# Embedding stages that multiply the unnormalized input, the next stage's sums of squares taken inside them, two normalizations in a row joined, and rotary angles computed behind the scaling

## The reference

```python
for i in range(DEPTH):                                   # 2 layers
    ...                                                  # layer 0: pooling; layer 1: attention (nsa)
    x = x + conv_ffn(rmsnorm(x, norm_ffn[i]), ...)
    gate = jax.nn.sigmoid(rmsnorm(x, norm_ple[i]) @ ple_gate[i])     # 1024 x 1024
    x = x + gate * (p[i] @ ple_proj[i])                  # p[i]: 256 tokens x 256, ple_proj: 256 x 1024
return rmsnorm(x, norm_final)

def rmsnorm(x, g):
    xf = x.astype(jnp.float32)
    y = xf * lax.rsqrt(jnp.mean(xf * xf, axis=-1, keepdims=True) + EPS) * g.astype(jnp.float32)
    return y.astype(x.dtype)
```

## Time and profile before

| | us |
|---|---|
| median of three runs | 2557.86 (2557.30 to 2558.94) |
| the profiled execution, its time | 2558.41 |
| its span in the trace | 2556.6 |
| ACT's first square of `ple0` to ACT's first square of `nsa` | 255.26 to 309.19 |
| ACT's first square of `nsa` to PE's first key matmul | 309.19 to 325.59 |
| ACT's first square of `ple1` to that of `norm_first` | 733.36 to 787.24 |
| `norm_first`, to the first square of `even_in` | 787.24 to 797.78 |
| first square of `even_in` to PE's first product there | 797.78 to 814.65 |

### The profile page before, as it was taken

The page is one execution under the profiler, slowest core; times in us unless marked ns, Lnnn a source line. Parts: engine busy times, 40 slices in busy tenths (PEclk is TensorE's granted clock), DMA queues, the critical chain, the costliest instruction groups (busy, mean ns, idle before and its releaser), DMA issues. The chain is left out here.

```text
span 2556.6 us, 36052 instructions
## 1 busy us (share of the span) xinstructions
PE 2193.2 (86%) x12176; PEld 1796.2 (70%) x12176; DVE 1681.2 (66%) x2815; ACT 1333.6 (52%) x2092; POOL 281.0 (11%) x355
## 2 busy tenths in 40 slices
PE   5999799989987999948887699995889986699994
PEld 4899676679974666737666687884678774577773
DVE  5884235368624479986663599995567754599994
ACT  2663214356423255656443388883476641488882
POOL 0000000000000056556100001101000000011100
PEclk8999899999988999969999699997898987699997
DMA  5554331456532766500021499996221111499992
GB/s 213 169 184 151 125 102 50 140 182 198 173 103 75 257 236 234 220 17 1 17 73 51 157 368 386 389 394 244 78 80 58 58 59 66 162 388 394 396 389 79
DMA packets 127254, 454.95 MB, mean 178 GB/s; under 512 B 13824, under 2 KB 17792, under 8 KB 126976
## 3 DMA queue, kind: packets, MB, share of 16 engines
q1 hardware_dynamic: 116160, 413.14, 44.5%
q0 software_dynamic: 10944, 39.85, 4.1%
HBM read 431.97 MB, written 20.97 MB: 177 GB/s over the span
## 5 line engine op out<-in xcount | busy, mean ns | idle before, releaser
L2525 DVE TENSOR_TENSOR moe_w_lo<-ring,moe_w_hi 128x1024 fp32r<-128x1024 f32 x384 | 462.7, 1222 | 62.4 <-ACT moe_w_hi L2463 57.4
L2463 ACT CAST moe_w_hi<-ring 128x1024 fp32r<-128x1024 f32 x384 | 399.0, 1049 | 147.6 <-PE ps L236 120.4
L373 DVE TENSOR_TENSOR ffn_w_lo<-ring,ffn_w_hi 128x1024 fp32r<-128x1024 f32 x132 | 161.0, 1223 | 101.6 <-ACT ffn_w_hi L325 101.4
L234 PE MATMUL ps<-moe_w_hi,moe_own 128*128 128x512 f32 x512 | 214.3, 419 | 12.1 <-DVE moe_own L2532 11.1
L235 PE MATMUL ps<-moe_w_lo,moe_own 128*128 128x512 f32 x512 | 205.1, 401 | 0.0
L236 PE MATMUL ps<-moe_w_hi,moe_own 128*128 128x512 f32 x512 | 205.0, 400 | 0.0
L325 ACT CAST ffn_w_hi<-ring 128x1024 fp32r<-128x1024 f32 x132 | 137.4, 1044 | 107.8 <-PE ps L236 107.8
L234 PE MATMUL ps<-ffn_h_hi,ffn_w_hi 128*128 128x256 f32 x608 | 173.3, 285 | 11.1 <-DVE ffn_w_lo L373 11.1
L235 PE MATMUL ps<-ffn_h_lo,ffn_w_hi 128*128 128x256 f32 x608 | 172.0, 283 | 0.0
L236 PE MATMUL ps<-ffn_h_hi,ffn_w_lo 128*128 128x256 f32 x608 | 172.0, 283 | 0.0
L2375 POOL DMA_INDIRECT moe_got<-token_rows,moe_idx x32 | 44.6, 1393 | 903.8 <-DVE moe_idx L2520 903.8
(11 more groups left out here) (487 smaller groups left out, 5487.9 us busy)
## 6 DMA issues: line engine op xcount, KB each, us to landing
ring<-in_weights SPq DMA_DIRECT2D x766, 512.0 KB, 5.3
expert_rows<-moe_y POOLq DMA_DIRECT2D x32, 512.0 KB, 7.3
token_rows<-moe_token_rows SPq DMA_DIRECT2D x6, 512.0 KB, 2.7
sq<-in_cmp_w SPq DMA_DIRECT2D x1, 2048.0 KB, 7.7
both<-in_x SPq DMA_DIRECT2D x1, 1024.0 KB, 5.8
both<-in_context SPq DMA_DIRECT2D x1, 1024.0 KB, 8.1
out<-both SPq DMA_DIRECT2D x1, 1024.0 KB, 4.8
cols<-in_cols SPq DMA_DIRECT2D x1, 720.5 KB, 9.2
```

The costliest lines, as they stand in the source:

```text
L234: pe.matmul(out, w_hi, x_hi, start=start, stop=False)
L373: dve.tensor_tensor(w_lo[:, u % WB], k.ring[:, (first + u) % RING], w_hi[:, u % WB], ALU.subtract).then_inc(w_split, 1)
L2463: act.copy(w_hi[:, j % WB].rearrange("p h f -> p (h f)"), k.slot(act, first + GU + j, e).rearrange("p a f -> p (a f)")).then_inc(w_rounded, 1)
L2525: dve.tensor_tensor(w_lo[:, j % WB].rearrange("p h f -> p (h f)"), k.ring[:, (first + GU + j) % RING].rearrange("p a f -> p (a f)"), w_hi[ ...
```

## The change

`ple` is rewritten, in both uses:

- The gates are multiplied from `x` times gain, without the reciprocal root; DVE multiplies each gate's sum by the reciprocal root afterwards (`apply_root`), and ACT applies the sigmoid to that.
- The first gate is a plain product on `k.h`; the other seven and the projection are products of parts. ACT casts nine ring slots (`cast`) and DVE subtracts (`split`), with three buffers; ACT and DVE also split `x` and `p`.
- The order on PE is gate 0, sums of squares, gates 1 and 2, projection, gates 3 to 7. The projection stays in its banks and DVE reads it from there.
- When tiles of the new `x` are there, ACT squares them (`next_square`) and PE adds them up (`next_sums`) for the next stage, in banks 6 and 7. At the end ACT takes a square root of no use in itself (L598), so that the table of the root is loaded when the next stage begins.
- `ple1` also squares and sums the context and takes its reciprocal root, and makes a second sum of squares of `x` weighted by `norm_final`, from which the root of both normalizations together follows.

`nsa` has no squares and sums any more; its root comes at once. DVE normalizes first and makes the angles after that; the factor on the cosine comes behind `shift_blocks`. The load into `sq` isn't held back. `final_norm("norm_first")` is gone. `even_in` reads both sums, normalizes `x` once with the joined gain and root, makes two of its first three weight splits between tiles, and writes the normalized `x` itself (8 tiles, with a reciprocal of its own) after its last split of the input.

```diff
+            def _(act):
+                def cast(i):
+                    if i >= WB:
+                        act.wait_ge(used, i - WB + 1)
+                    act.copy(w_hi[:, i % WB], k.slot(act, order[i])).then_inc(w_rounded, 1)
...
+                for t in range(KD):
+                    act.activation(k.sq[:, t, own], x[:, t, :], ACT.Square).then_inc(squared, 1)
+                cast(0)
+                for t in range(KD):
+                    act.mul(x_hi[:, t, :], x[:, t, :], gain[:, t:t + 1]).then_inc(x_rounded, 1)
...
+                act.wait_ge(summed, 1)
+                root(own, NORM_BANK).then_inc(rooted, 1)
...
+                for m in range(3, KD):
+                    if m + 4 < len(order):
+                        cast(m + 4)
+                    for t in (0, 1) if m == 3 else (m - 2,):
+                        next_square(t)
+                    sigmoid(m)
+                for t in (KD - 2, KD - 1):
+                    next_square(t)
+                act.activation(k.root[:, own], k.root[:, own], ACT.Sqrt)
...
+                for m in range(3, KD):
+                    if m + 4 < len(order):
+                        split(m + 4)
+                    apply_root(m)
+                    if m > 3:
+                        add(m - 1)
+                add(KD - 1)
...
-                dve.wait_ge(gated, m + 1)
-                    dve.wait_ge(kept, m + 1)
...
-                    sp.wait_ge(norm[1], 1)
                     sp.dma_start(w1[:, :, :, :], cmp_w1_in).then_inc(w1_loaded, 16)
...
-                    norm_scalar(k, act, norm, x, T)
+                    act.activation(k.root[:, 0:T], k.ps[:, SUM_BANK, 0:T], ACT.Sqrt, scale=1.0 / D, bias=k.eps[:, 0:1]).then_inc(rooted, 1)
...
+                for t in range(KD + 1):
+                    if t < KD:
+                        for part, g in ((other, gain[:, t, 0:1]), (own, both_gain[:, t:t + 1])):
+                            dve.scalar_tensor_tensor(k.h[:, t, part], x[:, t, part], g, k.rstd[:, part], ALU.mult, ALU.mult
+                                                     ).then_inc(made, 1)
...
+                    if 0 < t < WB:
+                        split(t)
+                dve.wait_ge(first_rooted, 1)
+                dve.reciprocal(k.rstd[:, other], k.root[:, other])
...
-        final_norm(k, x, col("norm_final"), "norm_first")
```

More of the change, by code:

```diff
@@ new lines, in next_sums @@
+                def next_sums(tiles):
+                    for t in tiles:
+                        pe.wait_ge(next_squared, t + 1)
+                        pe.matmul(k.ps[:, SUM_BANK, 0:T], k.ones[:, :], k.sq[:, t, own], start=(t == 0), stop=(t == KD - 1))
+                        if scale is not None:
+                            pe.matmul(k.ps[:, SCALED_BANK, 0:T], k.ones[:, :], k.sq[:, t, other], start=(t == 0), stop=(t == KD - 1))
+                w = k.slot(pe, gate_slots)
+                for t in range(KD):
+                    pe.wait_ge(x_scaled, t + 1)
+                    mm = pe.matmul(k.ps[:, 4, 0:T], w[:, t, :], k.h[:, t, own], start=(t == 0), stop=(t == KD - 1))
@@ new lines, in _ @@
+                mm.then_inc(product, 1)
+                for t in range(KD):
+                    pe.wait_ge(squared, t + 1)
+                    mm = pe.matmul(k.ps[:, NORM_BANK, 0:T], k.ones[:, :], k.sq[:, t, own], start=(t == 0), stop=(t == KD - 1))
+                mm.then_inc(summed, 1)
+                gates(1)
+                pe.wait_ge(scaled, 1)
+                gates(2)
+                project(0)
+                project(1)
+                if context is not None:
+                    for t in range(KD):
+                        pe.wait_ge(c_squared, t + 1)
+                        mm = pe.matmul(k.ps[:, SUM_BANK, 0:T], k.ones[:, :], k.sq[:, t, other], start=(t == 0), stop=(t == KD - 1))
+                    mm.then_inc(c_summed, 1)
@@ new lines, in next_square, with root @@
+                def next_square(t):
+                    act.wait_ge(added, t + 1)
+                    if scale is not None:
+                        act.activation(k.sq[:, t, other], x[:, t, :], ACT.Square, scale=weight[:, t:t + 1])
+                    act.activation(k.sq[:, t, own], x[:, t, :], ACT.Square).then_inc(next_squared, 1)
+                def root(part, bank):
+                    return act.activation(k.root[:, part], k.ps[:, bank, 0:T], ACT.Sqrt, scale=1.0 / D, bias=k.eps[:, 0:1])
@@ new lines, in _ @@
+                if scale is not None:
+                    act.drain()
+                    act.activation(weight[:, :], weight[:, :], ACT.Sqrt, bias=k.eps[:, 0:1])
+                    act.drain()
+                cast(1)
+                act.wait_ge(loaded, 16)
+                act.copy(pt_hi[:, :, :], pt[:, :, :]).then_inc(p_rounded, 1)
+                cast(2)
+                if context is not None:
+                    for t in range(KD):
+                        act.activation(k.sq[:, t, other], context[:, t, :], ACT.Square).then_inc(c_squared, 1)
@@ new lines, in _ @@
+                cast(3)
+                sigmoid(0)
+                cast(4)
+                sigmoid(1)
+                cast(5)
+                sigmoid(2)
+                if context is not None:
+                    act.wait_ge(c_summed, 1)
+                    root(other, SUM_BANK).then_inc(c_rooted, 1)
+                cast(6)
+                for m in range(3, KD):
[4 more added lines that the diff above has]
+                    sigmoid(m)
```

207 lines of the change are left out of this document (145 added, 62 removed).

## The result

| | median of the runs, us | range, n |
|---|---|---|
| before, run beside it | 2557.67 | 2557.3 to 2558.9, 4 |
| after | 2520.43 | 2513.41 to 2527.18, 4 |
| ratio | 0.9853 | 95%: 0.983 to 0.9876 |

The gain is 37.2 us where 50.8 were forecast. The median lies 13.4 us above the predicted 2507 and 0.4 above the end of the range. The span of the profiled execution went from 2556.6 to 2518.9.

A forecast was written before the change was run, and what follows sets the result against it. It took PE's waits in five stretches, the embedding stages and the starts of nsa and even_in, as the bound; 12.9 + 13.5 + 4.5 + 10.5 + 9.4 = 50.8 off 2557.9 gave 2507 us, range 2501 to 2520.

The forecast's parts named there:

- `ple0` with its turn: First embedding stage, from ACT's first square to the next stage: 41.0 us where it was 53.9, -12.9 us.
- `nsa`: Stage start: keys begin 2.9 us after it instead of 16.4, -13.5 us; slow first keys make no difference.
- `ple1` with its turn, and `norm_first`: Second embedding stage 49.4 us instead of 53.9, -4.5; the normalization stage goes whole, -10.5.
- `even_in`: PE's first product starts at 5.8 us, not 16.9; after added splits and handovers, -9.4 us.
- whatever reaches that stretch earlier ends earlier by as much: From 834 on PE is busy for all of 236 us at full clock, so earlier arrival carries through.
- My list of what would show me wrong: PE waiting at gates 3 to 7 over 3 us in a stage, or the stretch from 834 on lengthening.
- (a): PE falls to 1.2 GHz at the starts of both embedding stages, 2.9 us back in each: 2513; chance 0.12.
- (b): ACT and DVE pace the gates in both embedding stages, about 5 us each: 2517; chance 0.12.
- (c): In even_in's second product, DVE's 5.1 us of late normalization stand before PE in full: 2512; chance 0.06.
- (d): Five table loads in the embedding stages hold ACT longer than their rows, 6.4 us: 2513; chance 0.03.
- (e): Slower than before: PE's clock falls to 1.2 GHz in even_in's full 236 us, 2582 at 75 us; chance 0.02.
- (f): Late gates lose nothing, keys run at full clock, last table load is hidden; 5 us more: 2502; chance 0.06.

The follow-up runs named there:

- b_shift2: The kernel before, with nothing but a pause of 4.3 us between even_in and the scan stage ssd: 2569.12 us, ratio 1.0057.
- a_shift4: The changed kernel with a pause of 7.8 us (four reciprocals and a turn) between even_in and ssd: 2528.37 us, ratio 0.9871.
- a_fill: The changed kernel with unread matmuls put into PE's idle times of the scan stage ssd: 2508.47 us, ratio 0.9809.
- b_pad32: The kernel before with 32 matmuls of two columns at the program's start and nothing else: 2561.29 us, ratio 1.0018.
- a_fill_pad48: The changed kernel with the unread matmuls in ssd, plus 48 matmuls of two columns at the program's start: 2520.88 us, ratio 0.9864.
- second_half: The kernel before with only ple1, the joined normalization and even_in as changed, ple0 and nsa as before: 2547.98 us, ratio 0.9968.

## Where the prediction held, and where it failed

**The five terms held.** From the first square of `ple0` to the end of `even_in`:

| term | forecast | measured |
|---|---|---|
| `ple0` with its turn | -12.9 | -13.0 |
| `nsa` | -13.5 | -13.4 at the first key, -12.0 at the start of `ple1` |
| `ple1` with its turn, and `norm_first` | -15.0 | -14.9 |
| `even_in` | -9.4 | -10.0 |
| sum | -50.8 | -50.0 |

The one mis-sized term is `nsa`, by 1.4. I took the slow start of the keys for equal before and after, since PE has idled in both; it had 4.72 us of idle time now and 12.21 then, and yet the keys ran 1.14 us longer now, with 5.4 us of them at 1.2 GHz where it was 3.0. The angles behind the scaling cost nothing: `kcv` starts at 15.9 us in the stage where I had 16.1, and PE doesn't wait for it.

**The step that failed** is a sentence of the first part: "whatever reaches that stretch earlier ends earlier by as much". It is true of the stretch. I used it for all that lies behind it as well, and priced 1460 us of unchanged stages at nothing. Measured in its place, for the executions profiled: +5.8 in the scan up to `even_out` and some 1.6 of the 3.1 in `even_out` (half of low 12.8 against 9.7) by the clock; +6.1 by the two turns, in which PE's branch takes 3.35 and 3.49 us instead of 0.37 and 0.34; -3.9 in `hg`, whose low time is the same (50.1 against 50.0), but falls in part into the wait that went from 2.89 to 0.55. The other 1.4 of `even_out`'s 3.1 is a wait that the kernel before doesn't have:

```profile
1289.84 0.50 PE L234 MATMUL ps<-even_out_zs_hi,even_out_w_hi 128*128 128x512 f32 x1 [1.80 <-DVE even_out_w_lo L2270]
```

Behind `even_in` PE's low time went from 169.7 to 185.9 us. That the clock part goes with the place of the bursts and not with the change is shown by `b_shift2`, `a_shift4` and `a_fill`; that the turns go with the instructions' place, by `b_pad32`. What remains, 1.2 us, is spread over the other stretches. My list of what would show me wrong looked at the 236 full microseconds only, where nothing could happen.

**The rivals.**

(a) did not come: the first gate's 16 records took 3.69, 0.46 a matmul, and the clock is 1.00 from 255 to 296. The same mechanism came where I hadn't looked, in stages whose code is unchanged.

(b) did not come: behind the start of `ple0` PE has one wait, 1.37 us; in `ple1` it has 2.4 us in two waits for scaled gates, 1.5 the longer, and one of 0.5.

(c) did not come: from 774 to 784 PE is busy for 9.89 of 10 us.

(d) did not come. The scalings end at 258.63 + 3.29 = 261.92 and the load starts at 261.94; the last load of `ple0` ends at 294.94 and the root starts at 294.96. The Trainium skill, "ScalarE: Activation LUTs", section "What ACT_TABLE_LOAD costs", has a drain of about 1.4 us beside each load; of the eight loads of `ple0` and `ple1` seven have the next function within 0.03 us behind them and the eighth a wait for PE, and the stages took the time that the rows alone gave.

(e) did not come: 1.00 from 784 to 1020.

(f) did not come. The late gates lost nothing, but the keys weren't at full speed.

The range was too narrow for a reason that belongs in its working: no case in it was about the stages behind. From rows of before it could have been bounded: PE at 0.82 over 122 us of scan and 0.91 over 308 us of `hg` means low time of 18 and 50 us that may as well be 43 or 61, as other phases showed.

**What stays open.** What decides whether the clock falls at a given idle time; the rows show only that the same 1.70 us do it at one time and not at another. Whether PE's branch is long because the instructions behind it aren't there yet, and by which place in the program; no run moved the branch alone or took it out. Why PE's own time in `hg` is 1.3 us longer in the trace of the kernel before than in that of after. `a_fill_pad48` takes 4.1 us longer than `a_fill` from the first `kcv` to the next feed-forward stage, which is the clock again: low is 13.6 us there and 3.4.

## What to carry to other kernels

A gain worked out stage by stage holds at the end of the changed stages; whether it arrives at the end of the program is a second question, and its answer is in the stages that nobody touched. Look there for stretches where PE works in bursts with a granted clock between 0.5 and 1, and for branches over a stage's body, and widen the range by the time that they can lose; to test a change, compare marks at the end of what it touches, and run it once more with a small pause or a few idle instructions, so that the phase isn't taken for the effect. Once such a stage is known, a few unread matmuls in its waits can help to hold the clock: here the median went from 2520.4 to 2508.5, of which about 4 us are the scan's own; with some idle instructions at the start the same kernel took 2511.0 to 2520.9, so the rest is no sure gain.

## What the runs showed of the hardware

- PE's granted clock went to 1.2 GHz after idle times as short as 1.70 us in a burst-like stage at one place (0.51 over 1185 to 1189 in `after`), and didn't at the same place of the program in another kernel (1.00 over 1232.4 to 1236.4 in `before`); 697 identical matmuls took between 84.5 and 96.5 us of PE in the scan stages (`before` and `second_half`).
- With one and the same code ahead of the turn, the turn between two stages takes 2.4 to 2.6 us or 5.3 to 6.3 us, by a branch of PE that takes 0.34 to 0.37 or 3.3 to 3.9 us. 32 matmuls of two columns at the program's start added 3.1 us to each of two turns 1.8 and 2.5 ms later.
- PE at 1.2 GHz costs nothing in time that it would have waited: 24 matmuls of `hg` took 5.5 us instead of 3.1, and the wait behind them 0.55 instead of 2.89.
- A plain matmul of two columns, right behind the start, takes 0.43 us (20.64/48), as much as one of 256 columns in the middle of the kernel.
